# Upward strips of two MLPs: high and low activations side by side as one 512-column operand in four banks, the row factor squared at the residual, relu and square on ScalarE

## The chip, the core and the metric

One program runs on one core of one Trainium2 chip. The metric is device time in microseconds of one execution: a median over runs of 876.5 us (876.34 to 876.64) for the kernel before. Engines are named as the profile does: PE (TensorE matmul), PEld (its weight load), DVE (VectorE), ACT (ScalarE), POOL (GpSimd), SP (SyncE, which issues all transfers).

## The reference, cut to what matters

Two transformer blocks at 256 rows and width 1024, fp32. The change touches only the two MLPs, one at the end of each block (the second with `norm2_g`, `w_up_2`, `w_down_2`):

```python
a = jnp.square(jax.nn.relu(rms_norm(h, g_mlp[l]) @ w_up[l]))   # 256x1024 @ 1024x4096
h = h + a @ w_down[l]                                          # 256x4096 @ 4096x1024
# rms_norm(x, g) = x * rsqrt(mean(x*x, -1) + EPS) * g : one positive factor r per row
```

The factor r is positive, so relu(r·z)² = r²·relu(z)², and the factor of a row may stand before or behind both products.

## The kernel before, in words

**Number format.** Every large product is made from two rounded halves of each operand: x = x_hi + x_lo and w = w_hi + w_lo in a matmul type of reduced width, and x·w is taken as x_hi·w_hi + x_hi·w_lo + x_lo·w_hi: three matmuls (helper `three`, L1873 to 1880, every matmul at line L1878).

**Weight strips.** Weights are streamed in 65 strips of 2 MB, in two halves each. A half goes through four steps. SP loads it into one of three buffers `raw` (L599) once POOL has finished the half three before it. ACT copies it to `w_hi` (helper `hi`, L709 to 724) once PE is done with that half of the strip two before it, as there are two buffers `w_hi` and two `w_lo`. POOL makes `w_lo` = raw − w_hi (L680). PE multiplies. ACT, DVE and POOL execute in program order.

**An MLP** is 16 strips: eight upward, u0 to u7, each 512 columns of `w_up`, and eight downward, d0 to d7, each 512 rows of `w_down`, in the order u0, u1, d0, u2, d1, u3, ..., u7, d6, d7. The first MLP begins at strip 16 (`MLP1`), so u0 is strip 16, u1 is 17, d0 is 18, u2 is 19; after it comes strip 32 (`IN2`). The second begins at 49 (`MLP2`) and ends the program.

**An upward strip** has 4 blocks of 128 output columns times 8 blocks of the inner dimension, 32 steps of `three`; the weights are stationary and the 256 activation rows move: 96 matmuls of 256 columns, order x_hi with w_hi, x_lo with w_hi, x_hi with w_lo. Its output (128 x 1024) lies in two PSUM banks, 4 and 5 for even j, 6 and 7 for odd. A downward strip is 16 steps, 48 matmuls of 512 columns, accumulated over all d0 to d7 in banks 0 to 3.

**Between u_j and d_j** (DVE `activate`, L1469 to 1484): DVE waits for the strip, takes relu and the row factor in one instruction out of PSUM (L1475), squares it in place (L1480); ACT copies the square to `x_hi` (L930); DVE subtracts (L1484, `x_lo`), and that lets d_j start on PE. The factor rB is the row factor spread over columns: DVE makes a diagonal (L1197), PE multiplies it by ones in the middle of u1 (L2004), DVE takes it (L1208).

**ACT's order** in an MLP (L921 to 930): for i from 2 to 15 it makes both halves of `w_hi` of strip i, and behind them, where strip i−2 was a u_j, the copy to `x_hi` for j. So behind the halves of d0 comes the copy for u0, and then the halves of u2.

**The residual** (L1171 to 1190) adds the four banks to h, one instruction of 128x512 for each (L1177).

Of the kernel before, what the change touches and what calls it, by code (L numbers as in the profile page):

```python
# [20 lines left out]
S = 256  # L21
P = 128
NT = S // P
KT = D // P
# [56 lines left out]
def build(nc, a, out):  # L81
# [3 lines left out]
    with ctx:  # L85
        def sb(name, shape, dt=f32):
            return ctx.enter_context(nc.sbuf_tensor(name, shape, dt))

        def sem(name):
            return ctx.enter_context(nc.semaphore(name))  # L90
# [4 lines left out]
        LO = [sb(f"w_lo{i}", [P, 4096], f32r) for i in range(2)]  # L95
        XH = [sb(f"x_hi{i}", [P, 2048], f32r) for i in range(2)]
        XL = [sb(f"x_lo{i}", [P, 2048], f32r) for i in range(2)]
        xn = sb("xn", [P, NT, D])
# [55 lines left out]
        ta = AR[:, 14664:16200]  # L154
        act_q = AR[:, 14664:15688]
        comb2 = gbuf[1][:, 0:256]
        hg = u2[:, :, 1024:2048]
# [102 lines left out]
        up_evac = sem("up_evac")  # L260
        sq_ready = sem("sq_ready")
        a_hi, a_lo = sem("a_hi"), sem("a_lo")
# [160 lines left out]

        MLP_TURNS = FF // 512 // 2 - 1

        def up_strip(base, j):
# [261 lines left out]
        def _(act):  # L688
# [230 lines left out]
            fill_hi_between(17, lambda: row_stats(3, h, 2))  # L919

            def mlp(base, a0, abuf, before):  # L921
                for i in range(2, 16):
                    hi(base + i)
                    for j in range(8):
                        if up_strip(0, j) == i - 2:

                            act.wait_ge(sq_ready, a0 + j + 1)
                            act.wait_ge(strip_done, down_strip(base, j - 2) + 1 if j >= 2 else before)
                            c = slice(1024 * (j % 2), 1024 * (j % 2) + 1024)
                            nc.scalar.activation(XH[abuf][:, c], act_q, ACT.Copy).then_inc(a_hi, 1)  # L930

# [127 lines left out]
        def _(dve):  # L1059
# [110 lines left out]

            def residual(s, gain):  # L1171

                r = BANKED.index(s)
                for b in range(4):
                    t, c = b % 2, slice(512 * (b // 2), 512 * (b // 2) + 512)
                    bank_wait(r, b)
                    x = V.tensor_tensor(h[:, t, c], h[:, t, c], bank(b), ALU.add)  # L1177
                    if gain is None:
                        x.then_inc(res_done, 1)
                        continue  # L1180
                    link(x)
                    if b == 0 and s in GAIN_OF:
                        dve.wait_ge(gain_loaded[GAIN_OF[s]], 16)
                    V.tensor_tensor(xn[:, t, c], h[:, t, c], gain[:, c], ALU.mult).then_inc(xn_ready, 1)
                    if b >= 1:
                        fill_lo_block(b - 1)
                if gain is not None:
                    signal(evac_done, 1)
                    signal(src_ready, 1)
                    fill_lo_block(3)  # L1190

            def row_scale(i):

                dve.wait_ge(norm_sq, i + 1)
                newton(rstd_n[:, 2 * i:2 * i + 2], ss_n[:, 2 * i:2 * i + 2], y0_n[:, 2 * i:2 * i + 2], D)

            def rstd_diagonal(i):  # L1197
# [268 lines left out]
            row_scale(3)  # L1466
            broadcast_rstd(3, bank(0))

            def activate(j, done, a0, abuf, i=None):  # L1469

                def at(count, per_turn):
                    return count if i is None else i * per_turn + count

                dve.wait_ge(strip_done, at(done, 4))
                V.scalar_tensor_tensor(act_q.rearrange("p (c u) -> p c u", u=S),  # L1475
                                       bank(4 + 2 * (j % 2), 2).rearrange("p (c u) -> p c u", u=S), 0.0,
                                       bc(rB.unsqueeze(1), [P, 4, S]), ALU.max, ALU.mult).then_inc(up_evac, 1)
                n = a0 + j + 1
                dve.wait_ge(up_evac, at(n, 2))
                V.tensor_tensor(act_q, act_q, act_q, ALU.mult).then_inc(sq_ready, 1)  # L1480
                dve.wait_ge(sq_ready, at(n, 2))
                dve.wait_ge(a_hi, at(n, 2))
                c = slice(1024 * (j % 2), 1024 * (j % 2) + 1024)
                V.tensor_tensor(XL[abuf][:, c], act_q, XH[abuf][:, c].bitcast(f32), ALU.subtract).then_inc(a_lo, 1)  # L1484
                dve.wait_ge(a_lo, at(n, 2))
# [13 lines left out]
            def mlp(base, a0, abuf):  # L1499
                for j in (0, 1):  # L1500
                    activate(j, up_strip(base, j) + 1, a0, abuf)
                if base == MLP1:

                    dve.wait_ge(gain_loaded[4], 16)
                    dve.wait_ge(gain_loaded[5], 16)
                    link(V.tensor_tensor(g45, gbuf[0][:, :], gbuf[1][:, :], ALU.mult))
                with dve.Fori(0, MLP_TURNS) as i:
                    for j in (2, 3):
                        activate(j, up_strip(base, j) + 1, a0, abuf, i)

            mlp(MLP1, 0, 0)

            residual(IN2 - 1, g45)
            for b in range(4):
# [330 lines left out]
            row_scale(6)  # L1845
            broadcast_rstd(6, bank(0))
            mlp(MLP2, 8, 1)
            residual(NS - 1, None)


        @block.tensor
        def _(pe):
# [20 lines left out]
            def three(dst, xh, xl, wh, wl, start, stop, w_stationary):  # L1873
# [6 lines left out]
                return last  # L1880

            def steps_of(s):

                m = strips[s]["mode"]
                outer = NT if m == "tok" else 4
                inner = 4 if m in ("acc", "down", "mixed") else KT
                parts = 2 if s in HALVED else 1
                inner //= parts
                return [(o, inner * z + k) for z in range(parts) for o in range(outer) for k in range(inner)]

            def strip(s, first=0, last=None, fill_waits={}, i=None, evac_wait=True):
# [13 lines left out]
                if first == 0:  # L1905
# [3 lines left out]
                    if m == "up":  # L1909
                        if d["j"] >= 2 or ups[0] >= 8:  # L1910
                            pe.wait_ge(up_evac, at(ups[0] - 1, 2))
                        ups[0] += 1
# [4 lines left out]
                    if m == "down":  # L1917
                        a_n[0] += 1
                        pe.wait_ge(a_lo, at(a_n[0], 2))
                b0 = 4 + 2 * (d["j"] % 2) if m == "up" else d.get("pair", 0)  # L1920
                for n_step, (o, k) in enumerate(steps[first:last]):
# [6 lines left out]
                    if m == "tok":  # L1928
# [3 lines left out]
                                  hi_[:, c:c + w], lo_[:, c:c + w], k == 0, k == KT - 1, False)  # L1932
                    elif m in ("T", "up"):
                        c = 2048 * (k // 4) + w * (k % 4) + P * o
# [128 lines left out]
            def mlp_products(s0, s1):  # L2063
                filled_strip(s0)
                strip(s0 + 1, 0, 12)
                broadcast_rstd(bank(0))
                strip(s0 + 1, 12)
                pe.wait_ge(rb_taken, bcasts[0])
                strip(s0 + 2)
# [386 lines left out]
```

## Time and profile before

| | |
|---|---|
| time, median of 3 | 876.5 us (876.34 to 876.64) |
| span of the profiled execution | 874.3 us |
| the profiled execution's own time | not given apart from its span; the median of the runs lies 2.2 us above that span |
| PE busy | 865.4 us (99%) |
| PEld, POOL, DVE, ACT busy | 753.0, 679.1, 458.7, 429.2 us |
| mean transfer rate | 171 GB/s |

The span goes from the first to the last instruction. A busy share says how full an engine was, not whether it set the end: for that one looks at who waited for whom. Matmuls are pipelined, so the duration of one record is longer than the distance from one start to the next; rates are read from starts.

### The profile page before, as it was taken

To read this page: it belongs to the slowest core of one execution; us is meant where nothing else is said; L and a number is where in the kernel's file an instruction comes from. 1 tells how busy PE (TensorE), PEld (TensorE's weight loads), DVE (VectorE), ACT (ScalarE), POOL (GpSimd) and SP (SyncE) were. 2 spreads that over 40 slices of the span, in tenths; PEclk is the share of its full clock that TensorE was granted. 3 is DMA by queue.
4 is the path that set the end of the run, shared out by engine and by line. 5 is a ranking of instruction groups with operands and counts; after the bars stand their busy time and mean duration, and the time that the engine had idled before them with its cause. 6 is when DMAs were issued, how large, how long until landed. Compare 5 with 4: busy or idle time off the path is not lost.

```text
span 874.3 us, 13275 instructions
## 1 busy us (share of the span) xinstructions
PE 865.4 (99%) x5362; PEld 753.0 (86%) x5362; DVE 458.7 (52%) x666; ACT 429.2 (49%) x590; POOL 679.1 (78%) x389
## 2 busy tenths in 40 slices
PE   9999999999999999999999999999999999999998
PEld 7898887898899999998887797777788899999996
DVE  5697652423444221335788899559955552323233
ACT  6674486366354443343763645636455454434430
POOL 3789473958679999988898879812638889999881
PEclk9999999999999999999999999999999999999999
DMA  9865352534545666654854554520224446566531
GB/s 336 337 218 195 121 192 96 192 122 145 169 168 184 203 199 215 210 191 147 295 169 133 174 177 140 187 84 1 97 98 143 161 153 216 195 196 216 198 110 49
DMA packets 65555, 149.22 MB, mean 171 GB/s; under 512 B 4801, under 2 KB 10977, under 8 KB 65377
## 3 DMA queue, kind: packets, MB, share of 16 engines
q1 hardware_dynamic: 65504, 148.53, 50.8%
q8 instruction: 34, 0.56, 0.3%
q14 instruction: 17, 0.13, 0.0%
HBM read 147.47 MB, written 1.05 MB: 170 GB/s over the span
## 4 chain that ended last, share of the span: by engine, by line
PE 87%; DVE 6%; POOL 2%; ACT 2%; DMA 2%; issue 1%; SPq 0%; ACTq 0%; DVEq 0%
PE ps L1878 75%; PE ps L2059 2%; POOL w_lo L680 2%; PE ps L2033 2%; PE ps L1971 1%; PE ps L2045 1%; DMA h<-in_x 1%; PE ps L2305 1%; DVE xn L1768 1%; DVE arena L1321 1%; PE ps L2223 1%; PE ps L2244 1%; DMA raw<-in_w_in 1%; PE ps L2167 1%; PE ps L2012 0%
## 5 line engine op out<-in xcount | busy, mean ns | idle before, releaser
L680 POOL TENSOR_TENSOR w_lo<-raw,w_hi 128x512 fp32r<-128x512 f32 (+2 forms) x364 | 667.2, 1870 | 140.9 <-ACT w_hi L723 140.8
L723 ACT ACTIVATE w_hi<-raw 128x1024 fp32r<-128x1024 f32 (+3 forms) x193 | 247.8, 1321 | 255.4 <-PE ps L1878 119.4
L1878 PE MATMUL ps<-w_hi,x_hi 128*128 128x512 f32 (+1 forms) x672 | 266.8, 397 | 1.3 <-POOL w_lo L680 1.1
L1878 PE MATMUL ps<-w_hi,x_lo 128*128 128x512 f32 (+1 forms) x672 | 259.9, 387 | 0.0
L1878 PE MATMUL ps<-w_lo,x_hi 128*128 128x512 f32 (+1 forms) x672 | 259.8, 387 | 0.0
L1878 PE MATMUL ps<-x_hi,w_hi 128*128 128x256 f32 x704 | 201.7, 287 | 0.0
L1878 PE MATMUL ps<-x_hi,w_lo 128*128 128x256 f32 x704 | 199.3, 283 | 0.0
L1878 PE MATMUL ps<-x_lo,w_hi 128*128 128x256 f32 x704 | 199.2, 283 | 0.0
L1878 PEld LDWEIGHTS ps<-w_hi,x_hi 128*128 128x128 f32 x672 | 126.3, 188 | 33.4 <-issue 6.5
L1878 PEld LDWEIGHTS ps<-w_hi,x_lo 128*128 128x128 f32 x672 | 126.2, 188 | 25.8
L1878 PEld LDWEIGHTS ps<-w_lo,x_hi 128*128 128x128 f32 x672 | 126.4, 188 | 22.3
L1878 PEld LDWEIGHTS ps<-x_hi,w_hi 128*128 128x128 f32 x704 | 134.8, 191 | 2.3 <-issue 1.4
L1878 PEld LDWEIGHTS ps<-x_lo,w_hi 128*128 128x128 f32 x704 | 134.8, 192 | 0.7
L1878 PEld LDWEIGHTS ps<-x_hi,w_lo 128*128 128x128 f32 x704 | 134.8, 191 | 0.0
L1475 DVE SCALAR_TENSOR_TENSOR arena<-ps,arena 128x1024 f32<-128x1024 f32 x16 | 19.6, 1225 | 171.2 <-PE ps L1878 171.2
L1484 DVE TENSOR_TENSOR x_lo<-arena,x_hi 128x1024 fp32r<-128x1024 f32 x16 | 49.8, 3112 | 24.0 <-ACT x_hi L930 24.0
L769 ACT ACTIVATE arena<-ps,small 128x128 f32<-128x128 f32 (+1 forms) x80 | 32.8, 419 | 51.6 <-DVE small L1311 51.5
L1177 DVE TENSOR_TENSOR h<-h,ps 128x512 f32<-128x512 f32 x20 | 13.8, 688 | 51.3 <-PE ps L1878 51.2
L738 ACT ACTIVATE x_hi<-ps 128x512 fp32r<-128x512 f32 x24 | 14.2, 594 | 43.1 <-PE ps L1971 43.1
L2059 PE MATMUL ps<-arena 128*128 128x64 f32 (+1 forms) x240 | 31.1, 271 | 0.8 <-DVE gain L1761 0.7
L660 POOL TENSOR_TENSOR arena<-arena,small 128x768 f32<-128x768 f32 x2 | 3.0, 1498 | 35.7 <-DVE small L1075 35.7
L2059 PEld LDWEIGHTS ps<-arena 128*128 128x128 f32 x240 | 29.4, 192 | 1.6 <-issue 1.4
(285 smaller groups left out, 818.0 us busy)
## 6 DMA issues: line engine op xcount, KB each, us to landing
raw<-in_w_up SPq DMA_DIRECT2D x32, 1024.0 KB, 5.4
raw<-in_w_down SPq DMA_DIRECT2D x32, 1024.0 KB, 4.8
raw<-in_w_in SPq DMA_DIRECT2D x31, 1024.0 KB, 5.3
raw<-in_w_xkv SPq DMA_DIRECT2D x8, 1024.0 KB, 5.1
raw<-in_w_out SPq DMA_DIRECT2D x8, 1024.0 KB, 4.9
raw<-in_w_xq SPq DMA_DIRECT2D x4, 1024.0 KB, 5.1
raw<-in_w_xo SPq DMA_DIRECT2D x4, 1024.0 KB, 4.9
raw<-in_w_in SPq DMA_DIRECT2D x6, 512.0 KB, 7.9
```

The costliest lines, as they stand in the source:

```text
L680: x = nc.gpsimd.tensor_tensor(LO[s % 2][:, 2048 * q + d0:2048 * q + d1], RAW[n % 3][:, d0:d1], HI[s % 2][:, 2048 * q + d0:2048 * q + d1].b ...
L723: nc.scalar.activation(HI[s % 2][:, 2048 * q + c0:2048 * q + c1], RAW[n % 3][:, c0:c1], ACT.Copy).then_inc(hi_done, 1)
L738: nc.scalar.activation(dst[:, :, P * t:P * t + P], src, ACT.Copy).then_inc(tb_hi, 1)
L769: x = nc.scalar.activation(dst, sc[:, i // per, i % per, :], ACT.Exp, bias=nm[:, i // per, i % per:i % per + 1], accum_out=dn[:, i // per, ...
L1177: x = V.tensor_tensor(h[:, t, c], h[:, t, c], bank(b), ALU.add)
L1321: V.tensor_copy(u["pr"][2 + (i - 1) % 2][:, c], bank(6)[:, c]).then_inc(pt_done, 1)
L1475: V.scalar_tensor_tensor(act_q.rearrange("p (c u) -> p c u", u=S), bank(4 + 2 * (j % 2), 2).rearrange("p (c u) -> p c u", u=S), 0.0, bc(rB ...
L1484: V.tensor_tensor(XL[abuf][:, c], act_q, XH[abuf][:, c].bitcast(f32), ALU.subtract).then_inc(a_lo, 1)
L1768: link(V.tensor_tensor(y, y, wv[:, :, b], ALU.add))
L1878: last = T.matmul(dst, l, r, start=start and i == 0, stop=stop and i == 2, skip_group_check=w_stationary)
L2033: last = T.matmul(sc[:, r, k, :], q, kk, start=first, stop=x == len(qk) - 1, skip_group_check=True)
L2059: last = T.matmul(values_of(n)[:, sg["vw"] * si:sg["vw"] * si + sg["vw"]], pt[:, c:c + P], sg["v"][k], start=k == 0, stop=k == nk - 1)
```

## The change

Four edits, in both MLPs.

1. `x_hi` and `x_lo` become the two halves of one tile. A step of an upward strip is `both`: w_hi is loaded once and x_hi and x_lo move through it as one operand of 512 columns into one whole bank (hi·hi in its left half, lo·hi in its right); then w_lo with x_hi, 256 columns, is added to the left half. Four blocks take four banks: 0 to 3 for u0, 4 to 7 for every other.
2. ACT copies the right halves to SBUF (`up_second`), DVE adds the left halves (in `activate`), ACT takes relu and square and the copy to `x_hi` (`up_square`). DVE subtracts for `x_lo` as before.
3. The row factor is squared (`square_rstd`) and multiplied in at the residual; its broadcast by PE is gone.
4. ACT's order: `up_second` of j stands behind both halves of `w_hi` of the strip two behind u_j; `up_square` of j stands between the two halves of `w_hi` of the strip three behind it.

```diff
-        XH = [sb(f"x_hi{i}", [P, 2048], f32r) for i in range(2)]
-        XL = [sb(f"x_lo{i}", [P, 2048], f32r) for i in range(2)]
+        XB = [sb(f"x{i}", [P, 4096], f32r) for i in range(2)]
+        XH, XL = [x[:, 0:2048] for x in XB], [x[:, 2048:4096] for x in XB]
...
+        def up_bank(j):
+            return 0 if j == 0 else 4
...
+            def up_second(base, a0, j):
+                act.wait_ge(strip_done, up_strip(base, j) + 1)
+                src = bank(up_bank(j), 4).rearrange("p (c x) -> p c x", c=4)[:, :, S:2 * S]
+                nc.scalar.activation(act_c.rearrange("p (c u) -> p c u", u=S), src, ACT.Copy).then_inc(up_taken, 1)
+            def up_square(base, a0, j, abuf, before):
+                act.wait_ge(up_evac, a0 + j + 1)
+                link(nc.scalar.activation(act_c, act_q, ACT.Relu))
+                link(nc.scalar.activation(act_q, act_c, ACT.Square))
+                act.wait_ge(strip_done, down_strip(base, j - 2) + 1 if j >= 2 else before)
+                c = slice(1024 * (j % 2), 1024 * (j % 2) + 1024)
+                nc.scalar.activation(XH[abuf][:, c], act_q, ACT.Copy).then_inc(a_hi, 1)
             def mlp(base, a0, abuf, before):
+                j = 0
                 for i in range(2, 16):
-                    hi(base + i)
-                    for j in range(8):
-                        if up_strip(0, j) == i - 2:
-                            act.wait_ge(sq_ready, a0 + j + 1)
-                            act.wait_ge(strip_done, down_strip(base, j - 2) + 1 if j >= 2 else before)
-                            c = slice(1024 * (j % 2), 1024 * (j % 2) + 1024)
-                            nc.scalar.activation(XH[abuf][:, c], act_q, ACT.Copy).then_inc(a_hi, 1)
+                    hi(base + i, 0)
+                    if j and i - 3 == up_strip(0, j - 1):
+                        up_square(base, a0, j - 1, abuf, before)
+                    hi(base + i, 1)
+                    if j < 8 and i - 2 == up_strip(0, j):
+                        up_second(base, a0, j)
+                        j += 1
+                up_square(base, a0, 7, abuf, before)
...
+                        x = V.scalar_tensor_tensor(h[:, t, c], bank(b), rstd_n[:, 2 * scale + t:2 * scale + t + 1],
+                                                   h[:, t, c], ALU.mult, ALU.add)
...
-            broadcast_rstd(3, bank(0))
+            square_rstd(3)
...
-                dve.wait_ge(strip_done, at(done, 4))
-                V.scalar_tensor_tensor(act_q.rearrange("p (c u) -> p c u", u=S),
-                                       bank(4 + 2 * (j % 2), 2).rearrange("p (c u) -> p c u", u=S), 0.0,
-                                       bc(rB.unsqueeze(1), [P, 4, S]), ALU.max, ALU.mult).then_inc(up_evac, 1)
                 n = a0 + j + 1
-                dve.wait_ge(up_evac, at(n, 2))
-                V.tensor_tensor(act_q, act_q, act_q, ALU.mult).then_inc(sq_ready, 1)
-                dve.wait_ge(sq_ready, at(n, 2))
+                dve.wait_ge(up_taken, at(n, 2))
+                V.tensor_tensor(act_q.rearrange("p (c u) -> p c u", u=S),
+                                bank(up_bank(j), 4).rearrange("p (c x) -> p c x", c=4)[:, :, 0:S],
+                                act_c.rearrange("p (c u) -> p c u", u=S), ALU.add).then_inc(up_evac, 1)
                 dve.wait_ge(a_hi, at(n, 2))
...
+            def both(dst, xb, k, wh, wl, start, stop):
+                hl = xb.rearrange("p (z k u) -> p z k u", z=2, u=S)
+                T.matmul(dst, wh, hl[:, :, k, :], start=start, stop=stop, skip_group_check=True)
+                return T.matmul(dst[:, 0:S], wl, hl[:, 0, k, :], start=False, stop=stop, skip_group_check=True)
...
-                        if d["j"] >= 2 or ups[0] >= 8:
-                            pe.wait_ge(up_evac, at(ups[0] - 1, 2))
+                        if d["j"] >= 2:
+                            pe.wait_ge(up_evac, at(ups[0], 2))
...
-                strip(s0 + 1, 0, 12)
-                broadcast_rstd(bank(0))
-                strip(s0 + 1, 12)
-                pe.wait_ge(rb_taken, bcasts[0])
+                strip(s0 + 1)
```

## Rows read from the trace of the kernel before

**Rows 1.** The page: busy time, tenths by slice.
```profile
PE 865.4 (99%) x5362; PEld 753.0 (86%) x5362; DVE 458.7 (52%) x666; ACT 429.2 (49%) x590; POOL 679.1 (78%) x389
PEclk9999999999999999999999999999999999999999
```

**Rows 2.** Waits of PE, whole span: waiter, releaser, us in total, times, longest.
```profile
PE ps L1878 <- POOL w_lo L680: 1.1, 2, 0.8
```

**Rows 3.** Timeline of PE: start, duration, line; starts of u2, d1, u3.
```profile
270.17 0.28 PE L1878 MATMUL ps<-x_hi,w_hi 128*128 128x256 f32 x1
...
281.68 0.40 PE L1878 MATMUL ps<-w_hi,x_hi 128*128 128x512 f32 x1
...
292.59 0.28 PE L1878 MATMUL ps<-x_hi,w_hi 128*128 128x256 f32 x1
```

**Rows 4.** Timeline of PE: starts of u0 and d0 in both MLPs, and the broadcast.
```profile
235.29 0.36 PE L1878 MATMUL ps<-x_hi,w_hi 128*128 128x256 f32 x1
...
251.64 0.60 PE L2004 MATMUL ps<-arena,cst 128*128 128x256 f32 x2
...
252.19 0.28 PE L1878 MATMUL ps<-x_lo,w_hi 128*128 128x256 f32 x1
...
259.27 0.40 PE L1878 MATMUL ps<-w_hi,x_hi 128*128 128x512 f32 x1
...
714.63 0.40 PE L1878 MATMUL ps<-w_hi,x_hi 128*128 128x512 f32 x1
```

**Rows 5.** Timeline of ACT around u0, u1, d0; last field: idle before, released by.
```profile
244.73 5.59 ACT L723 ACTIVATE w_hi<-raw 128x2048 fp32r<-128x2048 f32 x4
255.25 1.06 ACT L930 ACTIVATE x_hi<-arena 128x1024 fp32r<-128x1024 f32 x1 [4.92 <-DVE arena L1480]
257.20 2.01 ACT L723 ACTIVATE w_hi<-raw 128x1024 fp32r<-128x1024 f32 x2 [0.89 <-DMA raw<-in_w_up]
...
712.66 2.01 ACT L723 ACTIVATE w_hi<-raw 128x1024 fp32r<-128x1024 f32 x2 [1.00 <-DMA raw<-in_w_up]
```

**Rows 6.** Timeline of SP: the load of u2's first half issued.
```profile
251.79 0.37 SPq L599 DMA_DIRECT2D raw<-in_w_up  x1
```

**Rows 7.** Timeline of DVE, the same stretch.
```profile
256.41 2.14 DVE L1484 TENSOR_TENSOR x_lo<-arena,x_hi 128x1024 fp32r<-128x1024 f32 x1 [1.20 <-ACT x_hi L930]
259.54 1.23 DVE L1475 SCALAR_TENSOR_TENSOR arena<-ps,arena 128x1024 f32<-128x1024 f32 x1 [0.99 <-PE ps L1878]
260.80 3.32 DVE L1480 TENSOR_TENSOR arena<-arena 128x1024 f32<-128x1024 f32 x1
```

**Rows 8.** Timeline of POOL: w_lo of d0, and of another strip (384.46).
```profile
251.73 2.39 POOL L680 TENSOR_TENSOR w_lo<-raw,w_hi 128x1024 fp32r<-128x1024 f32 x1
254.08 3.40 POOL L680 TENSOR_TENSOR w_lo<-raw,w_hi 128x1024 fp32r<-128x1024 f32 x1
257.43 5.60 POOL L680 TENSOR_TENSOR w_lo<-raw,w_hi 128x2048 fp32r<-128x2048 f32 x1
...
384.46 4.61 POOL L680 TENSOR_TENSOR w_lo<-raw,w_hi 128x2048 fp32r<-128x2048 f32 x1 [0.23 <-ACT w_hi L723]
```

**Rows 9.** Lines by source: duration in ns, min/median/max of DVE's instructions, ACT's out of PSUM.
```profile
L1475 DVE SCALAR_TENSOR_TENSOR arena<-ps,arena x16: 1223/1224/1227, 252.7 to 849.3; 128x1024 f32<-128x1024 f32 x16
L1484 DVE TENSOR_TENSOR x_lo<-arena,x_hi x16: 1379/2752/4375, 256.4 to 853.0; 128x1024 fp32r<-128x1024 f32 x16
L738 ACT ACTIVATE x_hi<-ps x24: 574/598/600, 165.8 to 694.2; 128x512 fp32r<-128x512 f32 x24
```

**Rows 10.** Timeline of ACT: w_hi of d7's second half; an ACT table load.
```profile
393.98 1.92 ACT L723 ACTIVATE w_hi<-raw 128x2048 fp32r<-128x2048 f32 x1 [3.75 <-PE ps L1878]
...
241.71 1.28 ACT L704 ACT_TABLE_LOAD   x1
```

**Rows 11.** Timeline of PE at the start: matmuls merged, duration of all, how many.
```profile
0.99 3.17 PE L1864 MATMUL ps<-idle_in 128*128 128x256 bf16 x14 [0.99 <-DVE idle_in L1217]
...
4.57 2.57 PE L1864 MATMUL ps<-idle_in 128*128 128x256 bf16 x22
```

More of the change, by code:

```diff
@@ L155, in build @@
         act_q = AR[:, 14664:15688]
+        act_c = AR[:, 0:1024]
         comb2 = gbuf[1][:, 0:256]
@@ L260, in build @@
         up_evac = sem("up_evac")
-        sq_ready = sem("sq_ready")
+        up_taken = sem("up_taken")
         a_hi, a_lo = sem("a_hi"), sem("a_lo")
@@ L1169, in scaled_copy, with residual @@
                 V.tensor_tensor(hg[:, t, c], h[:, t, c], gbuf[0][:, c], ALU.mult).then_inc(hg_ready, 1)
-            def residual(s, gain):
+            def residual(s, gain, scale=None):
                 r = BANKED.index(s)
@@ L1176, in residual @@
                     bank_wait(r, b)
-                    x = V.tensor_tensor(h[:, t, c], h[:, t, c], bank(b), ALU.add)
+                    if scale is None:
+                        x = V.tensor_tensor(h[:, t, c], h[:, t, c], bank(b), ALU.add)
+                    else:
+                        x = V.scalar_tensor_tensor(h[:, t, c], bank(b), rstd_n[:, 2 * scale + t:2 * scale + t + 1],
+                                                   h[:, t, c], ALU.mult, ALU.add)
                     if gain is None:
@@ L1195, in row_scale, with square_rstd @@
                 newton(rstd_n[:, 2 * i:2 * i + 2], ss_n[:, 2 * i:2 * i + 2], y0_n[:, 2 * i:2 * i + 2], D)
+            def square_rstd(i):
+                r = rstd_n[:, 2 * i:2 * i + 2]
+                link(V.tensor_tensor(r, r, r, ALU.mult))
             def rstd_diagonal(i):
@@ L1466, in _, with activate @@
             row_scale(3)
-            broadcast_rstd(3, bank(0))
-            def activate(j, done, a0, abuf, i=None):
+            square_rstd(3)
+            def activate(j, a0, abuf, i=None):
                 def at(count, per_turn):
                     return count if i is None else i * per_turn + count
-                dve.wait_ge(strip_done, at(done, 4))
-                V.scalar_tensor_tensor(act_q.rearrange("p (c u) -> p c u", u=S),
-                                       bank(4 + 2 * (j % 2), 2).rearrange("p (c u) -> p c u", u=S), 0.0,
-                                       bc(rB.unsqueeze(1), [P, 4, S]), ALU.max, ALU.mult).then_inc(up_evac, 1)
                 n = a0 + j + 1
-                dve.wait_ge(up_evac, at(n, 2))
-                V.tensor_tensor(act_q, act_q, act_q, ALU.mult).then_inc(sq_ready, 1)
-                dve.wait_ge(sq_ready, at(n, 2))
+                dve.wait_ge(up_taken, at(n, 2))
+                V.tensor_tensor(act_q.rearrange("p (c u) -> p c u", u=S),
+                                bank(up_bank(j), 4).rearrange("p (c x) -> p c x", c=4)[:, :, 0:S],
+                                act_c.rearrange("p (c u) -> p c u", u=S), ALU.add).then_inc(up_evac, 1)
                 dve.wait_ge(a_hi, at(n, 2))
@@ L1500, in mlp @@
                 for j in (0, 1):
-                    activate(j, up_strip(base, j) + 1, a0, abuf)
+                    activate(j, a0, abuf)
                 if base == MLP1:
@@ L1508, in mlp @@
                     for j in (2, 3):
-                        activate(j, up_strip(base, j) + 1, a0, abuf, i)
+                        activate(j, a0, abuf, i)
             mlp(MLP1, 0, 0)
-            residual(IN2 - 1, g45)
+            residual(IN2 - 1, g45, 3)
             for b in range(4):
@@ L1845, in _ @@
             row_scale(6)
-            broadcast_rstd(6, bank(0))
+            square_rstd(6)
             mlp(MLP2, 8, 1)
-            residual(NS - 1, None)
+            residual(NS - 1, None, 6)
         @block.tensor
@@ L1919, in strip @@
                         pe.wait_ge(a_lo, at(a_n[0], 2))
-                b0 = 4 + 2 * (d["j"] % 2) if m == "up" else d.get("pair", 0)
+                b0 = up_bank(d["j"]) if m == "up" else d.get("pair", 0)
                 for n_step, (o, k) in enumerate(steps[first:last]):
@@ L1932, in strip @@
                                   hi_[:, c:c + w], lo_[:, c:c + w], k == 0, k == KT - 1, False)
-                    elif m in ("T", "up"):
+                    elif m == "up":
+                        c = 2048 * (k // 4) + w * (k % 4) + P * o
+                        x = both(bank(b0 + o), XB[d["x"]], k, hi_[:, c:c + P], lo_[:, c:c + P], k == 0, k == KT - 1)
+                    elif m == "T":
                         c = 2048 * (k // 4) + w * (k % 4) + P * o
```

## The prediction, made before the changed kernel was run

> **What bounds the kernel now.** Read the page first. PE is busy 865.4 of 874.3 us and its clock stands at the upper of its two levels, 2.4 GHz, in every slice [rows 1]; POOL comes next with 679.1 us. Then the waits of PE: the longest entry over the whole span is 1.1 us [rows 2]. So PE sets the end, and a change pays by what it takes out of PE's stream, less each wait that it puts in front of PE. Third, the timeline of PE in the MLP, by starts: u2 takes 281.68 − 270.17 = 11.51 us for 96 matmuls, 0.120 us each; d1 takes 292.59 − 281.68 = 10.91 us for 48, 0.227 us each [rows 3]. A matmul costs its columns (107 ns per 256) and about 13 ns, so three small ones are worth little more than one large and one small. Last, the other engines at the head of an MLP, where PE's lead over them is small: this is where the forecast is made.
>
> **Part 1, the matmuls.** Of 32 steps of 3 × 0.120 = 0.360 us each remains 0.227 + 0.120 = 0.347 us, taking a 512-column operand in two pieces to be like the contiguous one of d1. A strip falls from 11.51 to 11.11 us, by 0.40 us [rows 3]; 16 strips: −6.5 us. Bounds: if all 13 ns of the dropped matmul went and nothing else changed, −6.8; if the split operand or the wider block cost its own 13 ns more per step, −6.5 + 512 × 0.013 = +0.2. I take −6.5.
>
> **Part 2, the broadcast.** In u1, PE's broadcast and the matmul behind it take 252.19 − 251.64 = 0.55 us where a matmul takes 0.12 [rows 4]: 0.43 us in each MLP, −0.9 us. It stands on PE's path and goes whole. DVE's share of it was covered by PE and counts nothing.
>
> **Part 3, the work between u_j and d_j.** ACT gains three instructions of 128x1024 per strip. Relu and square I price as the copy at L930, 1.06 us [rows 5]. The one out of PSUM: 128x512 takes 0.60 us, so between 1.05 and 1.2 [rows 9]; I take 1.06. DVE's add has one operand in PSUM and one in SBUF, as L1475 has, whose 16 instances all took 1.22 us; the subtraction, both operands in SBUF, took 1.38 to 4.37 [rows 9]. The rows show why: 256.41 + 2.14 = 258.55 is 1.07 us behind the end of POOL's instruction at 257.48, and 260.80 + 3.32 = 264.12 is 1.09 us behind the next end, 263.03 [rows 7, 8]. Such an instruction finishes 1.08 us after POOL's current one ends, and POOL's next is longer by 1.0 us (3.40 for 2.39, 5.60 for 4.61) [rows 8]. The square leaves DVE, so POOL gains about 1 us per strip. POOL does not hold PE, so that is worth nothing by itself.
>
> The Trainium skill ("ScalarE: Activation LUTs", Rules for kernel authors) advises VectorE, not ScalarE, for relu and multiplication. Here the fp32 square on DVE took 3.32 us beside POOL, against 1.06 us for an ACT instruction of that size [rows 5, 7]: this trace doesn't bear the advice out. By it the edit would only lengthen ACT's chain, which is counted next anyway.
>
> **Part 4, ACT's order, the step that decides.** Before, `x_hi` for u0 was made at 255.25, ahead of the halves of u2 [rows 5], `x_lo` was ready at 258.55 [rows 7], and d0 could start at 259.27 without waiting [rows 4]: 0.7 us to spare. Now relu, square and copy for u0 stand behind the first half of `w_hi` of u2. That waits for its transfer, issued at 251.79 when POOL finished the half three before [rows 6], and ran 257.20 to 259.21 [rows 5]. None of this depends on what changes, so:
> - u0 and u1 end 2 × 0.40 + 0.43 = 1.24 us earlier: PE is at d0 at 258.03 instead of 259.27.
> - ACT: 259.2 + 3 × 1.06 = 262.4.
> - POOL, without the stretch by the square: 254.08 + 2.40 = 256.5, + 4.61 = 261.1, + 2.40 = 263.5 [rows 8]. DVE's subtraction, begun at 262.5, ends 1.08 us later: 264.5.
> - PE waits 264.5 − 258.0 = 6.5 us.
>
> The second MLP has the same picture: `w_hi` of u2 at 712.66 [rows 5] instead of 257.20, d0 at 714.63 [rows 4]; PE at d0 at 713.4, `x_lo` at 719.9, a wait of 6.5 us. Together +13.0. The bounds of a wait: with an unhindered subtraction (1.22) 263.7 − 258.0 = 5.7; with the longest (4.37) 8.8. Queued behind the late x_hi on ACT are only the second half of u2 and `up_second` of u1. That half landed before at 263.12 at the latest, and ACT is free for it at 262.4; u2 isn't due before 275. Nobody else is late.
>
> Is the wait given back? No: in steady state PE is the slower side (22.02 us a pair of strips, POOL 4 × 2.40 + 2 × 4.61 + 1.0 = 19.8 [rows 8]), so what PE loses stays lost.
>
> **The other strips.** u_j ends; ACT makes one half (1.92), takes the right halves (1.06), DVE adds (1.22), then ACT 3 × 1.06, DVE subtracts. For u7, after which only d6 stands in between, from 393.98 [rows 10]: 395.9, 397.0, 398.2, 401.4, 402.8 with POOL idle, against d7 due at 393.8 + 10.9 = 404.7. 1.9 us to spare; with a subtraction of 4.37 it would be 1.2 us late, +0 to +2.4 for both; I take 0. For the others the order leaves a strip more. u_j+1 waits for the add on u_j, done during d_j−1: hidden. At the residual, an instruction with a factor instead of an addition, 128x512 each out of PSUM: no change. Squaring the factor is 0.2 us on DVE during u1.
>
> **Part 5, the clock.** No wait of PE at its weight strips is longer than 0.8 us [rows 2]. At the start, after idling, it issued 14 matmuls of 256 columns in 3.17 us, 0.213 us apart, and from 4.57 us on 22 in 2.57 us, 0.109 us apart [rows 11]. The first distance is that of 1.2 GHz, the second of 2.4. So 3.6 us of work ran at half speed, at a cost of 1.8 us. I expect that a wait of 6.5 us lets the clock fall and that d0 pays the same, +1.8 us in each MLP, +3.6. Bounds: 0, if it doesn't fall; twice that, +7.2.
>
> The Trainium skill ("TensorE: Matmul & The Clock Gate", Part 1) says that the half rate is the default and activity releases it, and that idle time brings it back. No stretch of this trace has PE idle long enough to show it; the sum above rests on the first microseconds.
>
> **Sum,** against the span of 874.3: −6.5 − 0.9 + 13.0 + 3.6 = +9.2, 883.5. The median lies 2.2 us above the span; with that offset unchanged, 885.7 us.
>
> **The rivals.**
> - A, the wait comes but the clock doesn't fall: +5.6, 882.1 us. For it: rows 11 show a start from rest, not a fall after work. Against it: 6.5 us is many times the pauses that it stood. 15%.
> - B, the wait costs less than PE saves, and the kernel is faster. The savings per MLP are 8 × 0.40 + 0.43 = 3.7 us; so the point of decision is `x_lo` for u0 ready by 261.7. That takes u2's first half in `raw` some 3 us sooner. For it: ACT's idle time before was put down to that transfer [rows 5]. Against: its issue at 251.79 hangs on POOL's work on u1, which nothing here shortens. With no wait at all the time is 876.5 − 7.4 = 869.1 us. 9%.
> - C, relu or square each bring a table load of 1.28 us [rows 10] before them: two in each `up_square`, 2.6 us more before d0 and 0.7 us late before d7, +6.6 in all, 892.3 us. Against it: the squares of the row statistics run behind copies without a load. 4%.
> - D, more is late than I see: the clock costs double, the subtraction takes 4.37 us at both heads, or the split operand costs 13 ns: each +4 to +7, some 891 us. 14%.
> - That the change doesn't do what it says (matmuls without any gain, and the waits as forecast) is in D.
>
> **How the numbers follow.** My own case 58%, at 885.7 (884 to 888). The range leaves out B, C and the far part of D: 881.0 to 890.5. About 0.2% (1.8 us) is what can be told from no change. Faster: B less its cases near zero, 7%; same 4%; slower 89%.
>
> **What would show it.** In the profile of the changed kernel: 32 steps of u2 in 11.1 us; a wait of PE for the subtraction of about 6.5 us, twice, at d0 and nowhere else; matmuls of d0 about 0.43 us apart at first, then 0.227; POOL's instructions stretched once, not twice, per pair. It would be wrong if d0 starts before 262 in the first MLP, or if u2 keeps its 11.5 us.

## The result and the profile after

The changed kernel takes 895.78 us (895.18 to 896.17, 4 runs), the kernel before beside it 876.57 us (876.34 to 877.02, 4 runs): ratio 1.0216 [1.0201, 1.023], slower by 19.2 us. The forecast was 885.7 us, range 881.0 to 890.5: the direction was right, the size was not, and the time lies outside the range. The span of the profiled execution grew from 874.3 to 893.9 us, by 19.6 where the sum said 9.2; the median lies 1.9 us above this span, where the forecast took 2.2. From here lines of the new kernel are cited: L1905 is `three`, L1912 and L1913 the wide and the narrow matmul of `both`, L1506 and L1511 DVE's addition and subtraction, L930 to L939 ACT's instructions between u_j and d_j.

The page's head, against [rows 1]: PE's share fell from 99% to 97% although it works no less, and its clock is below the upper level in two slices of 40.

```profile
PE 866.5 (97%) x4846; PEld 728.1 (81%) x4846; DVE 406.4 (45%) x646; ACT 476.5 (53%) x638; POOL 656.4 (73%) x389
PEclk9999999999989999999999999999999979999999
```

The waits of PE, against [rows 2] (waiter, releaser, us in total, times, longest):

```profile
PE ps L1905 <- DVE x L1511: 19.0, 2, 13.1
PE ps L1905 <- POOL w_lo L685: 1.1, 2, 0.8
```

A new entry of 19.0 us stands there, in two waits that are not alike: 5.9 and 13.1. The timeline of PE, against [rows 3, 4] (start, duration, line, shapes, idle before with releaser), shows them at d0 of either MLP; between them are the starts of u2, d1 and u3:

```profile
258.37 0.28 PE L1913 MATMUL ps<-x,w_lo 128*128 128x256 f32 x1
264.58 0.77 PE L1905 MATMUL ps<-w_hi,x 128*128 128x512 f32 x1 [5.93 <-DVE x L1511]
...
278.25 0.39 PE L1912 MATMUL ps<-x,w_hi 128*128 128x512 f32 x1
...
289.54 0.40 PE L1905 MATMUL ps<-w_hi,x 128*128 128x512 f32 x1
...
300.48 0.39 PE L1912 MATMUL ps<-x,w_hi 128*128 128x512 f32 x1
...
732.88 0.77 PE L1905 MATMUL ps<-w_hi,x 128*128 128x512 f32 x1 [13.08 <-DVE x L1511]
```

The chain of waits in front of the first one (start, duration, what) is the forecast step for step: transfer, first half of `w_hi` of u2, relu, square, copy, subtraction.

```profile
251.83 5.30 DMA raw<-in_w_up
...
257.21 2.00 ACT w_hi L728 x2
259.22 0.96 ACT arena L935
...
260.20 1.07 ACT arena L936
...
261.29 1.07 ACT x L939
...
262.38 2.07 DVE x L1511
264.44 0.14 issue
264.58 3.75 PE ps L1905 x8
```

In the second MLP ACT's part is the same (718.67 to 723.80) and only the last link differs. The timeline of DVE, both subtractions for u0:

```profile
262.38 2.06 DVE L1511 TENSOR_TENSOR x<-arena,x 128x1024 fp32r<-128x1024 f32 x1 [9.79 <-ACT x L939]
...
723.83 8.90 DVE L1511 TENSOR_TENSOR x<-arena,x 128x1024 fp32r<-128x1024 f32 x1 [9.72 <-ACT x L939]
```

And POOL's, beside them:

```profile
260.99 2.36 POOL L685 TENSOR_TENSOR w_lo<-raw,w_hi 128x1024 fp32r<-128x1024 f32 x1
263.29 3.38 POOL L685 TENSOR_TENSOR w_lo<-raw,w_hi 128x1024 fp32r<-128x1024 f32 x1
...
722.53 2.36 POOL L685 TENSOR_TENSOR w_lo<-raw,w_hi 128x1024 fp32r<-128x1024 f32 x1
724.84 2.35 POOL L685 TENSOR_TENSOR w_lo<-raw,w_hi 128x1024 fp32r<-128x1024 f32 x1
727.15 4.50 POOL L685 TENSOR_TENSOR w_lo<-raw,w_hi 128x2048 fp32r<-128x2048 f32 x1
```

Read the ends. In the first MLP the subtraction waited for the end at 263.35 and finished 1.09 us behind it, and POOL's next was stretched to 3.38: the picture of [rows 7, 8]. In the second it began at 723.83 under an instruction that ended at 724.89. POOL then ran two more at their plain length (2.35, 4.50), the last ended at 731.65, and the subtraction finished at 732.73, 1.08 us behind that one, when POOL had nothing queued. It passed over two ends at which it could have got in.

The Trainium skill ("SBUF — State Buffer", Who interferes with whom) says that VectorE's tensor_tensor with both inputs in SBUF contends with GpSimd's reads, that the port pair the two share is an exclusive lock, and that issue order decides who blocks. The trace agrees with the first two: the addition at L1506, with one input in PSUM, took 1.22 us all 16 times, the subtraction up to 8.90 in the same kernel, and wherever POOL worked beside it, it ended 1.08 or 1.09 us behind the end of a POOL instruction. Against the third, POOL's two instructions at 724.84 and 727.15 went ahead of a subtraction begun at 723.83.

### The profile page after: what moved, and what is told of

Read it like the earlier page. It is cut to its first block, busy times and chain, and to the rows that moved or that the text cites. A ratio compares the mean times of both kernels' runs of the same rounds, so it can differ in the third digit from the quotient of the medians.

```text
span 893.9 us, 12235 instructions
## 1 busy us (share of the span) xinstructions
PE 866.5 (97%) x4846; PEld 728.1 (81%) x4846; DVE 406.4 (45%) x646; ACT 476.5 (53%) x638; POOL 656.4 (73%) x389
## 4 chain that ended last, share of the span: by engine, by line
PE 81%; DVE 8%; ACT 4%; POOL 3%; DMA 3%; issue 2%; SPq 0%; ACTq 0%; DVEq 0%
PE ps L1905 53%; PE ps L1912 10%; PE ps L1913 5%; POOL w_lo L685 3%; PE ps L2095 2%; PE ps L2069 2%; ACT w_hi L728 1%; DVE x L1511 1%; DMA raw<-in_w_up 1%; PE ps L2007 1%; PE ps L2081 1%; DMA h<-in_x 1%; PE ps L2338 1%; ACT arena L706 1%; DVE arena L1351 1%
## 5 line engine op out<-in xcount | busy, mean ns | idle before, releaser
L1905 PE MATMUL ps<-w_hi,x 128*128 128x512 f32 (+1 forms) x1344 | 435.1, 395 | 20.3 <-DVE x L1511 19.0
L1905 PEld LDWEIGHTS ps<-w_hi,x 128*128 128x128 f32 x1344 | 253.8, 190 | 80.6 <-issue 26.0
L1905 PE MATMUL ps<-w_lo,x 128*128 128x512 f32 (+1 forms) x672 | 261.6, 389 | 0.0
L1912 PE MATMUL ps<-x,w_hi 128*128 128x512 f32 x512 | 181.4, 398 | 0.0
L1905 PEld LDWEIGHTS ps<-w_lo,x 128*128 128x128 f32 x672 | 127.7, 190 | 22.9
L1913 PE MATMUL ps<-x,w_lo 128*128 128x256 f32 x512 | 143.5, 280 | 0.0
L1912 PEld LDWEIGHTS ps<-x,w_hi 128*128 128x128 f32 x512 | 96.2, 188 | 23.5
L1913 PEld LDWEIGHTS ps<-x,w_lo 128*128 128x128 f32 x512 | 96.6, 189 | 0.5
L1506 DVE TENSOR_TENSOR arena<-ps,arena 128x1024 f32<-128x1024 f32 x16 | 19.6, 1225 | 160.7 <-ACT arena L930 160.7
L1511 DVE TENSOR_TENSOR x<-arena,x 128x1024 fp32r<-128x1024 f32 x16 | 35.4, 2211 | 116.1 <-ACT x L939 116.1
L1905 PE MATMUL ps<-x,w_hi 128*128 128x256 f32 x384 | 71.5, 287 | 0.0
L1905 PEld LDWEIGHTS ps<-x,w_hi 128*128 128x128 f32 x384 | 59.9, 191 | 1.9 <-issue 1.4
L1905 PE MATMUL ps<-x,w_lo 128*128 128x256 f32 x192 | 54.3, 283 | 0.0
L1905 PEld LDWEIGHTS ps<-x,w_lo 128*128 128x128 f32 x192 | 36.6, 191 | 0.0
```

The source lines that it names most:

```text
L1506: V.tensor_tensor(act_q.rearrange("p (c u) -> p c u", u=S), bank(up_bank(j), 4).rearrange("p (c x) -> p c x", c=4)[:, :, 0:S], act_c.rearr ...
L1905: last = T.matmul(dst, l, r, start=start and i == 0, stop=stop and i == 2, skip_group_check=w_stationary)
L1912: T.matmul(dst, wh, hl[:, :, k, :], start=start, stop=stop, skip_group_check=True)
L1913: return T.matmul(dst[:, 0:S], wl, hl[:, 0, k, :], start=False, stop=stop, skip_group_check=True)
```

## The experiments

The theory after this reading: (1) ACT's order makes the two waits; (2) the subtraction stands behind POOL and can lose several ends; (3) the clock falls in both waits and costs some 5 us; (4) the strip gains 0.22 us and not 0.40. Rivals: a chance event in one execution, the place of the tiles in SBUF, a cost of the operand in two pieces. The diffs below are against the changed kernel where nothing else is said. Lines that an edit adds shift the numbers behind them: in such kernels the subtraction is L1513 and `three` L1907 or L1909.

**The changed kernel again, without an edit.**

> The changed kernel once more, unaltered. If the 8.90 us subtraction before d0 of the second MLP belongs to the kernel (an order of events that comes out the same way each time), it stands here again, span 893.5 to 894.2 us. If it is chance, the subtraction ends 1.08 us behind the first end of a POOL instruction, some 6.6 us earlier, and the span is about 887 us.

895.94 us (1 run). The second MLP's subtraction took 8.71 us, the first's 2.15, and PE waited 13.1 us again. It belongs to the kernel.

**ACT's order.** `up_square` of u0 goes in front of the halves of u2.

```diff
                 for i in range(2, 16):
+                    if i == 3:
+                        up_square(base, a0, 0, abuf, before)
                     hi(base + i, 0)
-                    if j and i - 3 == up_strip(0, j - 1):
+                    if j > 1 and i - 3 == up_strip(0, j - 1):
```

> Relu, square and copy for u0 go ahead of the first half of w_hi of u2 instead of behind it; nothing else. Theory (ACT's order makes PE wait at d0, and the waits make the clock fall): x_lo for u0 is ready at about 257.6 us in the first MLP, before PE gets to d0 at 258.5; no wait, no fall of the clock; the time is that of before less the gains in PE's stream: 876.5 - 16 x 0.22 - 0.9 + 0.5 = 872.6 us. Rival 1 (the subtraction starves beside POOL as it did in the second MLP): PE still waits 3 to 5 us at one d0 or both, 877 to 884 us. Rival 2 (the order isn't the cause): 895.8 us.

Median 871.64 us of 10 runs; six lie at 871.2 to 871.8, the others at 879.7, 880.9, 882.4 and 893.1; ratio 0.9968 [0.9935, 1.0002]. By the median that is 4.9 us under the kernel before; the ratio's interval, which takes in three of the long ones, still reaches no change. No wait at d0 is left: without the order neither wait arises. The profiled execution is one of the long ones (879.67), and shows what happened in it (waits of PE, then DVE and the POOL work beside it):

```profile
PE ps L2009 <- DVE xn L1211: 5.7, 1, 5.7
```

```profile
161.79 8.71 POOL L685 TENSOR_TENSOR w_lo<-raw,w_hi 128x512 fp32r<-128x512 f32 x7
162.73 0.69 DVE L1201 TENSOR_TENSOR h<-h,ps 128x512 f32<-128x512 f32 x1 [12.42 <-PE ps L1907]
163.45 7.59 DVE L1211 TENSOR_TENSOR xn<-h,gain 128x512 f32<-128x512 f32 x1
```

It is the same loss in a place that no edit touches, ahead of the MLPs: a DVE instruction with both operands in SBUF, whose 12 instances have a median of 0.69 us, took 7.59 while POOL ran a row of seven (its end is 161.79 + 8.71 = 170.50; the addition finished 0.54 us behind). So the loss is not bound to the heads of the MLPs, and it doesn't come in every execution. The other three long ones were not profiled.

**PE kept busy in the wait.** Dummy matmuls stand in front of d0, up to about where the subtraction ends.

```diff
                 strip(s0 + 1)
+                pe.wait_ge(up_evac, 1 if s1 == IN2 else 9)
+                keep_busy(0, 50 if s1 == IN2 else 110)
                 strip(s0 + 2)
```

> Before d0 PE waits for the add on u0 and then issues idle matmuls into a free bank, 50 in the first MLP (5.4 us) and 110 in the second (12 us), so that it is busy for most of its wait; nothing else. Theory (d0 is long, 13.67 and 13.37 us for 10.94, because the clock fell while PE idled): both are 10.94 again and the time falls by 2.7 + 2.4 = 5.1 us to 890.7 us. Rival (d0 is long for another reason, such as weights that come late): d0 stays long, 895.8 us.

891.16 us (890.59 to 891.86, 4 runs), ratio 1.0166 [1.0149, 1.0182]: 4.6 us less than the changed kernel (5.1 by the spans of the two profiles), with the same lateness. Busy time in windows (us; busy of PE, PEld, DVE, ACT, POOL with counts; granted clock as a share of full; transfers), first the changed kernel over d0 of both MLPs:

```profile
264.58:268.00 3.42, 3.42 (x8) 2.74 (x9) 1.23 (x1) 0.47 (x1) 3.42 (x2) 0.50 0.39 97
264.58:270.00 5.42, 5.42 (x13) 4.26 (x14) 1.23 (x1) 0.47 (x1) 5.42 (x2) 0.50 0.55 181
271.00:278.24 7.24, 7.24 (x33) 6.00 (x32) 0.06 (x1) 5.08 (x5) 4.29 (x3) 1.00 0.47 147
...
732.88:746.24 13.36, 13.36 (x48) 10.83 (x49) 1.17 (x2) 5.08 (x5) 4.10 (x2) 0.81 0.21 76
```

and the one kept busy:

```profile
264.58:275.54 10.96, 10.96 (x48) 9.09 (x49) 1.28 (x2) 5.43 (x6) 10.79 (x4) 1.00 0.64 210
```

d0 starts at the same 264.58 in both. It takes 278.25 − 264.58 = 13.67 us after an idle PE, 10.96 after a busy one. The clock was at its lower level, 1.2 GHz, for the first 5.4 us of d0 and back at the upper one, 2.4 GHz, from 271.00 on. The cost is 2.7 us in the first MLP and, 13.36 against 11.00 with PE kept busy, 2.4 in the second.

The Trainium skill ("TensorE: Matmul & The Clock Gate", Part 1) has the half rate as the default state that activity releases. The windows agree: 0.50 behind a pause of 5.93 us, 1.00 where the pause was filled.

**POOL held off.** w_lo of u2 waits until the subtraction for u0 is done.

```diff
                         pool.wait_ge(hi_done, HI_COUNT[s, q, i])
+                        if s in (MLP1 + 3, MLP2 + 3) and q == 0 and i == 0:
+                            pool.wait_ge(a_lo, 1 if s == MLP1 + 3 else 9)
```

> POOL doesn't begin w_lo of u2 until the subtraction for u0 is done, so that DVE has its port alone; nothing else. Theory (the subtraction starves beside POOL): it takes 1.2 us or ends 1.1 us behind POOL's w_lo of d0 in both MLPs; PE's wait at d0 is 5.4 to 5.9 us in each, 0.5 less in the first and 7.5 less in the second, 887.5 us; the wait of POOL is hidden, as it is the faster side. Rival (DVE was held by something other than POOL, the transfers or ACT): the subtraction still takes 8.9 us in the second MLP and the time is 895 us or more.

887.76 us (885.51 to 888.3, 4 runs), ratio 1.0119 [1.0101, 1.0137]. The source line of the subtraction (duration in ns, min/median/max), then the waits of PE:

```profile
L1513 DVE TENSOR_TENSOR x<-arena,x x16: 1225/1824/1824, 262.2 to 868.1; 128x1024 fp32r<-128x1024 f32 x16
```

```profile
PE ps L1907 <- DVE x L1513: 10.6, 2, 5.3
```

With POOL idle the subtraction takes 1.23 us at both heads and the waits are 5.3 us each. Both are near the lower bound that the prediction gave (5.7). Even so the kernel is 11 us behind the kernel before: what is left is ACT's order and the clock. POOL's two pauses cost PE nothing that can be seen: its waits for POOL at the weight strips total 0.8 us here, 1.1 without the pauses.

**Smaller POOL instructions.** If the subtraction gets in at one of POOL's ends, more ends should help; if it waits till POOL runs dry, they should not.

```diff
-                        size = 2048 if MLP1 + 2 <= s < IN2 or s >= MLP2 + 2 else 512
+                        size = 2048 if MLP1 + 4 <= s < IN2 or s >= MLP2 + 4 else 512
```

> POOL makes w_lo of d0 and u2 in pieces of 512 columns instead of 1024 and 2048, in both MLPs; nothing else, the pieces of ACT included. Theory 1 (the subtraction waits for any gap that it wins between two POOL instructions, and more gaps mean more chances): it takes 1.3 to 2.5 us in both MLPs; the time falls by 6.5 us or so to 889 us. Theory 2 (once it has lost, it waits until POOL's queue is empty): it still takes 8 to 10 us in the second MLP, 896 us.

904.57 us (896.13 to 904.92, 4 runs), ratio 1.0268 [1.0206, 1.0331]. DVE and POOL in the first MLP:

```profile
260.58 11.05 POOL L685 TENSOR_TENSOR w_lo<-raw,w_hi 128x512 fp32r<-128x512 f32 x9
262.43 10.28 DVE L1511 TENSOR_TENSOR x<-arena,x 128x1024 fp32r<-128x1024 f32 x1 [9.71 <-ACT x L939]
```

```profile
PE ps L1905 <- DVE x L1511: 28.5, 2, 14.5
```

POOL's row of nine ended at 271.63, the subtraction at 272.71. It began under the second of the nine, let seven ends pass, and only the end of the row let it in. In the second MLP it took 10.29 us. In this run the theory of the empty queue holds, and its price was taken too low, since both MLPs were struck. As a rule it isn't safe: in the profile of ACT's order a later subtraction let an end pass that came 0.06 us after its start, and got in at the next although POOL's following instruction, stretched to 5.60, was there at once:

```profile
322.32 3.50 DVE L1513 TENSOR_TENSOR x<-arena,x 128x1024 fp32r<-128x1024 f32 x1 [6.60 <-ACT x L939]
322.35 2.39 POOL L685 TENSOR_TENSOR w_lo<-raw,w_hi 128x1024 fp32r<-128x1024 f32 x1
324.71 5.60 POOL L685 TENSOR_TENSOR w_lo<-raw,w_hi 128x2048 fp32r<-128x2048 f32 x1
```

One of the four runs, at 896.13, was about 8 us shorter; it has no profile, but that is what one MLP without the loss would give.

**The two activation tiles in each other's place.**

```diff
-        XB = [sb(f"x{i}", [P, 4096], f32r) for i in range(2)]
+        XB = [sb(f"x{i}", [P, 4096], f32r) for i in (1, 0)][::-1]
```

> The two tiles that hold x_hi and x_lo change places in SBUF; nothing else. If the place of the operands decides who wins between DVE and POOL, the long subtraction goes from the second MLP to the first or goes away (889 us or less). If it is the sequence of events in the second MLP, it stays at 8 to 9 us there: 895.8 us.

893.72 and 888.58 us (2 runs). The first was profiled and has 8.68 us in the second MLP and 2.02 in the first, as without the swap. So the swap doesn't take the loss away in every execution. The second run was 5 us shorter, with a mean granted clock of 0.992 against 0.989, as when POOL was held off (0.992); it has no profile, so whether it escaped the loss, and whether the swap has a part in that, stays open.

**The wide operand out of one piece.** On top of ACT's order above; the product is another, as the expectation says.

```diff
-                T.matmul(dst, wh, hl[:, :, k, :], start=start, stop=stop, skip_group_check=True)
+                T.matmul(dst, wh, xb[:, 512 * (k // 2):512 * (k // 2) + 512], start=start, stop=stop, skip_group_check=True)
```

> With ACT's order of e1_order, the 512-column matmul of an upward strip reads 512 adjacent columns (of x_hi alone, so that its products are of other operands) instead of two pieces of 256 that lie 2048 apart. Theory (the operand in two pieces costs 9 ns per matmul, as the distances 0.236 and 0.227 us of the traces suggest): 32 steps take 11.11 us instead of 11.29, and an undisturbed execution 871.5 - 16 x 0.18 = 868.7 us. Rival (the alternation of 512 and 256 columns costs it, or the writing of a whole bank): 11.29 us stays.

872.57 us (1 run), and u2 still takes 304.41 − 293.12 = 11.29 us:

```profile
293.12 0.39 PE L1914 MATMUL ps<-x,w_hi 128*128 128x512 f32 x1
...
304.41 0.40 PE L1907 MATMUL ps<-w_hi,x 128*128 128x512 f32 x1
```

The cost isn't the operand's two pieces; this theory of mine fell. The same profile has another loss away from the heads, in a strip with time to spare, where PE doesn't wait for it: two ends passed, and the subtraction got in behind the third.

```profile
315.29 8.10 DVE L1513 TENSOR_TENSOR x<-arena,x 128x1024 fp32r<-128x1024 f32 x1 [6.60 <-ACT x L939]
```

**ACT's order with a guard against POOL.** On top of ACT's order, the second half of w_lo of d0 waits for the subtraction, so that only one piece of POOL's work can stand in front of it.

```diff
                         pool.wait_ge(hi_done, HI_COUNT[s, q, i])
+                        if s in (MLP1 + 2, MLP2 + 2) and q == 1:
+                            pool.wait_ge(a_lo, 1 if s == MLP1 + 2 else 9)
```

> ACT's order of e1_order, and POOL begins the second half of w_lo of d0 only when the subtraction for u0 is done, in both MLPs, so that the two can't contend at d0. Theory: the subtraction ends at about 257.6 us as in e1_order, PE doesn't wait at d0, POOL loses under 0.2 us against e1_order as it would have been stretched by 1.0 us anyway; undisturbed executions take 871.5 us. Where e1_order's slow executions (879.7 to 893.1 us) come from the contention at d0 they are gone; where they come from the additions before the MLP, as its profile shows, they remain, at 877 to 884 us.

871.22 us (870.73 to 871.88, 9 runs), ratio 0.9924 [0.9898, 0.9951] (0.994 by the medians, as two of the 14 runs of the kernel before were long ones), and no long execution in nine. That the guard keeps them away isn't shown: the next two kernels have it too, and have 3 and 2 long ones in 12. PE goes from u1 into d0 without a pause, and its longest wait at a weight strip is 0.7 us:

```profile
258.69 0.28 PE L1917 MATMUL ps<-x,w_lo 128*128 128x256 f32 x1
258.81 0.40 PE L1909 MATMUL ps<-w_hi,x 128*128 128x512 f32 x1
```

```profile
PE ps L1909 <- POOL w_lo L687: 1.0, 2, 0.7
```

This version beats both kernels: 5.3 us under the kernel before, 24.6 under the change as it was made, by the medians. Strips (16 × 0.22 = 3.5) and broadcast (1.2, below) explain 4.7 of the 5.3; I didn't follow the rest.

**Four wide, then four narrow.** On top of the last. In the changed kernel a wide and a narrow matmul alternate; if the change of width is what costs, grouping should bring a strip to 11.15 us.

```diff
-                T.matmul(dst, wh, hl[:, :, k, :], start=start, stop=stop, skip_group_check=True)
-                return T.matmul(dst[:, 0:S], wl, hl[:, 0, k, :], start=False, stop=stop, skip_group_check=True)
+                for n in range(4):
+                    T.matmul(dst, wh[n], hl[:, :, k + n, :], start=start and n == 0, stop=stop and n == 3, skip_group_check=True)
+                for n in range(4):
+                    last = T.matmul(dst[:, 0:S], wl[n], hl[:, 0, k + n, :], start=False, stop=stop and n == 3, skip_group_check=True)
```

> On e7_gated_order: in an upward strip the four steps of one output block and half are issued as four matmuls of 512 columns with w_hi and then four of 256 with w_lo, instead of 512 and 256 in turn. Theory (a 512-column matmul followed by a 256-column one takes 0.236 us where one followed by its like takes 0.227): four steps take 3 x 0.227 + 0.236 + 3 x 0.120 + 0.117 = 1.394 us instead of 1.411, a strip 11.15 us instead of 11.29, and the time falls by 2.2 us to 869.0 us. Rival (each 512-column matmul of these strips costs 0.236 us whatever follows): no change, 871.2 us.

Median 869.95 us of 12 runs (nine near 869.9, three at 879 to 880), ratio 0.9953 [0.9925, 0.9981]. The strip takes 302.73 − 291.53 = 11.20 us, between the 11.15 of the theory and the 11.29 of its rival:

```profile
291.53 1.07 PE L1917 MATMUL ps<-x,w_hi 128*128 128x512 f32 x4
292.44 0.64 PE L1919 MATMUL ps<-x,w_lo 128*128 128x256 f32 x4
292.91 1.09 PE L1917 MATMUL ps<-x,w_hi 128*128 128x512 f32 x4
293.84 0.63 PE L1919 MATMUL ps<-x,w_lo 128*128 128x256 f32 x4
...
302.73 0.40 PE L1909 MATMUL ps<-w_hi,x 128*128 128x512 f32 x1
```

Grouping gives back half of what was missing, 0.09 us a strip and 1.3 us in all. But by the distances the cost doesn't sit at the change of width. From 266 to 400 us of this profile, a wide matmul of an upward strip is on average 0.233 us before the next wide one and 0.229 before a narrow one, where the theory had 0.227 and 0.236. Why a wide one costs more there than the 0.227 of a downward strip stays open. This kernel is the fastest here by its median. Its three long executions are as long as those of ACT's order; they weren't profiled.

**The wide matmul as two narrow ones.** On top of the guarded order: all that the change does, but three narrow matmuls a step as before.

```diff
-                T.matmul(dst, wh, hl[:, :, k, :], start=start, stop=stop, skip_group_check=True)
+                T.matmul(dst[:, 0:S], wh, hl[:, 0, k, :], start=start, stop=stop, skip_group_check=True)
+                T.matmul(dst[:, S:2 * S], wh, hl[:, 1, k, :], start=False, stop=stop, skip_group_check=True)
```

> On e7_gated_order: the 512-column matmul is taken apart into two of 256 columns with w_hi, into the same bank; all else stays, the four banks, ACT's part and the row factor. It measures the worth of the wide matmul by itself. Theory (by distances of the traces): a strip takes 11.51 us instead of 11.29, 16 x 0.22 = 3.6 us more, 874.8 us. Rival (something beside PE sets the pace of the strips): under 1 us of difference.

Median 874.95 us (874.37 to 882.87, 12 runs, two of them over 878), ratio 0.9992 [0.9976, 1.0009]. The strip is back at 303.55 − 292.04 = 11.51 us:

```profile
292.04 0.28 PE L1916 MATMUL ps<-x,w_hi 128*128 128x256 f32 x1
...
303.55 0.40 PE L1909 MATMUL ps<-w_hi,x 128*128 128x512 f32 x1
```

So the wide matmul alone is worth 874.95 − 871.22 = 3.7 us, against 16 × 0.22 = 3.5 by the strips. (The kernel before took 876.49 us beside this one and 876.52 beside the other, so the two can be compared.)

## Why the prediction was right about the sign and wrong about the size

The steps of the forecast against the profiled execution, in us:

| step | forecast | measured | from |
|---|---|---|---|
| part 1, the matmuls | −6.5 | −3.5 | u2 11.29, 16 × (11.51 − 11.29) |
| part 2, the broadcast | −0.9 | −1.2 | u0's start to the time due for d0: 23.98 to 23.13 and 23.97 to 22.76, less 2 × 0.22 each |
| part 4, wait in MLP 1 | +6.5 | +6.1 | 264.58 − 258.49 |
| part 4, wait in MLP 2 | +6.5 | +13.2 | 13.08 idle and one distance |
| part 5, the clock | +3.6 | +5.1 | 2.7 + 2.4, d0 with PE idle and with PE kept busy |
| downward strips | 0 | +0.5 | d1 10.94 for 10.91, 16 × 0.03 |
| given back between the MLPs | 0 | −0.8 | the strip behind MLP 1 starts 7.0 later, u0 of MLP 2 only 6.2 |
| sum | +9.2 | +19.4 | span: +19.6 |

(The time due for d0 is the last start of u1 and one distance of 0.12: 258.37 and 258.49 in the first MLP, 719.52 and 719.64 in the second. u0 starts at 235.36 and 696.88, before at 235.29 [rows 4] and 690.66.)

**The step that failed** is part 4, in the sentence that DVE's subtraction "ends 1.08 us later" than POOL's next end, which rests on part 3: "Such an instruction finishes 1.08 us after POOL's current one ends". In all 16 subtractions of before it did. In the second MLP, which the forecast took to have "the same picture", it let two more POOL instructions pass and took 8.90 us. The bound of 4.37 was the longest of 16 cases that had all got in at the first end, and no bound on losing. This step alone, 13.2 for 6.5, is 6.7 of the 10.4 us by which the sum for the span was missed. The run with POOL held off (1.23 us, waits of 5.3) shows that the time is contention with POOL, and the small pieces (10.28, seven ends lost) show that it can last until POOL has nothing left to do. Why this subtraction lost and the one in the first MLP didn't stays open.

**Part 1** was right in kind and mis-sized: +3.0 us. The step was priced at 0.227 + 0.120 from strips in which every matmul has the same width; alternating, it takes 11.29 / 32 = 0.353 us. The kernel with three narrow matmuls confirms that the strip's gain is the wide matmul's, the operand out of one piece shows that two pieces cost nothing, and grouping gave back half of what was missing, 0.09 of 0.18 us a strip. The cause of the other half is open, and so is how the first half comes about.

**Part 5** was right that the clock falls and mis-sized: +5.1 for +3.6, inside its bounds. I took the cost of a start from rest, 3.6 us of work at the lower level; here it was 5.4 us and more, as the window 264.58:270.00 at 0.50 shows.

Part 2 gave 0.4 us in the first MLP, as forecast, and 0.8 in the second. Of the sums that weren't tested, the lateness of d7 with a subtraction of 4.37 comes out at 401.4 + 4.37 − 404.7 = 1.1 us and not 1.2; nothing hangs on it.

**What held:** ACT's order as the cause, the chain in front of the first d0 to 0.1 us (264.44 forecast as 264.5), relu and square at 1.04 to 1.06 us without a table load (rival C), no lateness at any other strip. Rival B, the faster kernel, was wrong for this order. But its mechanism is right: with `x_lo` ready in time the median is 871.2, near the 869.1 that it gave; the 3.0 us that part 1 was short are more than the difference. Rival D had the right kind (a longer subtraction at the heads) with too small a price, and it stood just outside my range. The tail of that case should have been inside it.

## What to carry to other kernels

When an instruction of another engine is put behind a transfer-bound one, price the wait at the place with the smallest lead, and count the clock that falls with it; a saving spread over 16 strips was eaten by two waits. A VectorE instruction with both operands in SBUF on the critical path isn't bounded by the next end of GpSimd's work (8.90 us here, where 1.23 would do): give it a PSUM operand (1.22 us all 16 times) or hold GpSimd's next instruction behind it, and don't take the longest instance seen as its worst. A cost read from a stream of equal matmuls is not quite the cost in a mixed one.

## What the runs showed of the hardware that was not expected

- DVE's instruction with two SBUF operands can lose to POOL instructions that start behind it: 8.68 to 8.90 us in four profiles of the changed order, 8.10 at a later strip of a fifth profile, 10.28 with short pieces, 1.23 with POOL idle. What decides whether it gets in at an end stays open. The time from its start to POOL's next end doesn't tell the cases apart: at the head of the first MLP it was 0.93 to 1.10 us and the subtraction got in, at the head of the second 0.83 to 1.06 us and it didn't (four profiles). Shorter pieces of POOL's work didn't help.
- The same loss occurs, in one profiled execution, at an addition that takes 0.69 us elsewhere (7.59); that execution is 8 us longer than the undisturbed ones. That the kernel before has long executions too (884.16 and 885.05 among 14) is seen; that they, and the long ones without a profile, have this cause isn't shown.
- A matmul's price isn't settled by its width. 512 columns took 0.227 us in downward strips, also in front of a matmul of 256 (six cases before the change), and in upward strips 0.236 when alternating with 256 (0.117) and 0.232 on average when grouped by four.
